# First layer of a two-layer streaming encoder: products of x times the norm's weight, the norm's factor multiplied onto the product tiles, and another order of gates and y products

## The chip, the cores and the metric

The kernel runs on one core of a Trainium2 chip. The metric is the device time of one execution in microseconds. TensorE does the matmuls, ScalarE the activation functions, VectorE elementwise work and scans, GpSimd elementwise work; SyncE issues most DMAs. Each engine works through its own list of instructions in order; between engines there are semaphores.

## What is computed

The reference runs two layers for 1024 frames of a new stream and 64 frames of a running one. Only the first layer's mixer is touched here:

```python
def rmsnorm(x, g):
    y = x * rsqrt(mean(x * x, axis=-1) + 1e-6)
    return y * g

def lru_mixer(h, conv_buf, h0, ...):          # h = rmsnorm(x, norm_mix[0])
    gate = gelu(h @ w_y + b_y)
    u, new_buf = causal_dwconv(h @ w_x + b_x, conv_buf, conv_w, conv_b)   # 4 taps
    r = sigmoid(block_diag(u, ga_w, ga_b))
    i = sigmoid(block_diag(u, gx_w, gx_b))
    log_a = -8.0 * r * softplus(-lam)
    a = exp(log_a)
    bx = sqrt(-expm1(2.0 * log_a)) * (i * u)
    hs = scan(h_t = a_t * h_{t-1} + bx_t), starting from h0
    return (hs * gate) @ w_out + b_out, new_buf, hs[:, -1]
```

Behind it come a residual, a causal ConvFFN, a second layer (RWKV-7 mixing and another ConvFFN) and a last norm. All sizes are fp32: D_MODEL 1024, so 8 channel tiles of 128.

## The kernel before

Activations lie transposed: a tile is 128 channels by 1092 columns (1024 frames, 4 columns of gap, 64 frames), and x is 8 such tiles (X). A matmul takes 364 columns, so a tile is three. Each fp32 product is made of three: operands are split into a high part and a rest (`WH`, `WL` for weights, `HH`, `HL` for rows of h, `PH`, `PL` for rows going into the output projection). ScalarE writes the high parts (`w_hi`, `h_hi`, `p_hi`), GpSimd the rests of weights and of the projection's rows (`w_lo`, `p_lo`), VectorE the rests of h. An **up product** (`up`, L1236) is one tile of output: 8 tiles of input by 3 parts by 3 column blocks, 72 matmuls. A **down product** is one output tile of the projection for two channel tiles: 18 matmuls; `down` (L1263) makes eight. Products go in turn into two accumulators in PSUM, `ACC[0]` and `ACC[1]`; who has emptied one says so with `taken0` or `taken1`, and TensorE waits for that before it writes there again.

The head (before the first product): SyncE issues four small priming loads, the vectors V, the constants CO, the eight tiles of x, and two weight tiles (L332 to L340). `norm` on ScalarE (L510) squares each x tile as it lands, VectorE adds the squares up (L1698), TensorE sums over channels with a matrix of ones (L1275), ScalarE takes the root by Ln and Exp. Then `h_rows` (L1715) on VectorE writes x times weight times factor, ScalarE the high part, VectorE the rest, and `up_two` (L1244) makes the first two x products together, tile by tile.

The recurrent block runs in four groups of two channel tiles, f = 2g and 2g+1. In a group before, TensorE made: x product, x product, y product, gates of f, y product, gates of f+1, and from group 1 on the eight down products of the group before (g-1). `gates` (L1303) are two products of a 128 by 128 block by the convolved tile, in full fp32. ScalarE empties x products into `UB` (row 0 of T, with bias), y products through Gelu into rows 2 and 3, and the gate products through Sigmoid into rows 4 and 5; behind the sigmoids come Tanh, Exp and Sqrt, each with a table load. VectorE runs `lru_conv` (L1780: three one-column copies of history, a copy of the state, a TENSOR_SCALAR and three taps), `drive` (gate times convolved tile), `scale` (two steps behind the root), `run_on` (fill, copy, scan), `gated` (a copy of the state and the product of scan and y tile), and takes the down products onto X (`take`, L1734). Rows of T are shared by the channels (R, I, S, Q are rows 4 to 7), so ScalarE waits for `conv` or `p_lo` before it overwrites one. Weights come through two buffers: a weight is loaded when `w_lo` of the one before the last is done, and its high part is written once the product that used the buffer is finished.

The later norm, ahead of the first layer's ConvFFN, is already made the other way: products of x times weight, and the factor `RS` multiplied onto the product tiles; `inverse_root` (L533), `scaled_hi` (L529), `scaled_lo` (L1709) and `sums_of_squares` (L1287) belong to it.

## Time and profile before

| | us |
|---|---|
| three runs, median | 3187.39 |
| lowest, highest | 3183.47, 3194.0 |
| the profiled execution | 3185.53 |
| its span | 3183.7 |
| TensorE busy in the span | 3013.1 |
| end of the touched stretch (sum of squares of the next norm) | 408 |

The profile is of one execution. Its timeline gives each instruction or run of like instructions with start and length, and in brackets how long the engine was idle before and what ended that. The table of stretches gives busy times between two points in time and the clock that TensorE was granted (1.0 is 2.4 GHz, 0.5 is 1.2 GHz). The groups add up instructions of a line and shape.

### The profile page before, as it was taken

To read this page: it belongs to the slowest core of one execution; us is meant where nothing else is said; L and a number is where in the kernel's file an instruction comes from. 1 tells how busy PE (TensorE), PEld (TensorE's weight loads), DVE (VectorE), ACT (ScalarE), POOL (GpSimd) and SP (SyncE) were. 2 spreads that over 40 slices of the span, in tenths; PEclk is the share of its full clock that TensorE was granted. 3 is DMA by queue.
4 is the path that set the end of the run, shared out by engine and by line. 5 is a ranking of instruction groups with operands and counts; after the bars stand their busy time and mean duration, and the time that the engine had idled before them with its cause. 6 is when DMAs were issued, how large, how long until landed. Compare 5 with 4: busy or idle time off the path is not lost.

```text
span 3183.7 us, 66664 instructions
## 1 busy us (share of the span) xinstructions
PE 3013.1 (95%) x29240; PEld 2894.2 (91%) x29240; DVE 1760.1 (55%) x1821; ACT 1027.6 (32%) x1269; POOL 968.3 (30%) x549
## 2 busy tenths in 40 slices
PE   6999899999999999879997999998999999999997
PEld 5898899999999999879996777887999999999996
DVE  5555665556555557512205777773566555555566
ACT  4633521111111112544315777774311111111112
POOL 1222122222322224313313555652132222222221
PEclk9999999999999999999998999999999999999998
DMA  3111011111111111052232222212111111111111
GB/s 104 37 43 44 27 47 41 47 41 46 41 47 47 41 47 40 28 217 89 83 123 63 72 72 70 72 50 97 48 41 48 40 47 47 41 47 41 46 47 63
DMA packets 87531, 185.65 MB, mean 58 GB/s; under 512 B 28896, under 2 KB 51936, under 8 KB 87264
## 3 DMA queue, kind: packets, MB, share of 16 engines
q1 hardware_dynamic: 80352, 154.73, 15.4%
q10 hardware_dynamic: 6912, 26.84, 2.1%
q8 instruction: 231, 3.78, 0.5%
q14 instruction: 36, 0.29, 0.0%
HBM read 145.01 MB, written 36.53 MB: 57 GB/s over the span
## 4 chain that ended last, share of the span: by engine, by line
PE 79%; DVE 12%; ACT 5%; issue 1%; POOL 1%; DMA 1%; ACTq 0%; SPq 0%; DVEq 0%; POOLq 0%
PE PS L1230 66%; PE PS L1426 9%; DVE T L1676 2%; DVE X L1676 2%; PE PS L1361 2%; DVE T L1691 2%; ACT T L492 1%; DVE BK L1676 1%; PE PS L1258 1%; DVE HL L1686 1%; DVE G L1676 1%; ACT UV L492 1%; ACT L492 1%; DVE T L1681 1%; DVE T L1686 1%
## 5 line engine op out<-in xcount | busy, mean ns | idle before, releaser
L1011 POOL TENSOR_TENSOR WL<-RAW,WH 128x1024 fp32r<-128x1024 f32 x204 | 497.4, 2438 | 1454.9 <-ACT WH L492 1451.0
L1230 PE MATMUL PS<-HH,WH 128*128 128x364 f32 x3408 | 757.6, 330 | 28.1 <-DVE HL L1676 12.5
L1230 PE MATMUL PS<-HH,WL 128*128 128x364 f32 x3408 | 756.5, 330 | 0.0
L1230 PE MATMUL PS<-HL,WH 128*128 128x364 f32 x3408 | 752.9, 329 | 0.0
L1230 PEld LDWEIGHTS PS<-HH,WH 128*128 128x128 f32 x3408 | 591.7, 188 | 36.4 <-DVE HL L1676 12.2
L1230 PEld LDWEIGHTS PS<-HH,WL 128*128 128x128 f32 x3408 | 596.9, 189 | 0.0
L1230 PEld LDWEIGHTS PS<-HL,WH 128*128 128x128 f32 x3408 | 593.8, 189 | 0.0
L492 ACT ACTIVATE WH<-RAW 128x1024 fp32r<-128x1024 f32 x204 | 216.5, 1061 | 766.2 <-PE PS L1230 752.8
L1676 DVE TENSOR_TENSOR X<-PS,X 128x1092 f32<-128x1092 f32 x224 | 290.1, 1295 | 234.2 <-PE PS L1230 228.4
L1676 DVE TENSOR_TENSOR T<-PS,T 128x1092 f32<-128x1092 f32 x96 | 124.3, 1295 | 529.3 <-PE PS L1230 517.3
L1230 PE MATMUL PS<-PH,WH 128*128 128x364 f32 x1344 | 300.8, 332 | 20.8 <-ACT T L492 7.8
L1230 PE MATMUL PS<-PL,WH 128*128 128x364 f32 x1344 | 298.3, 330 | 0.0
L1230 PE MATMUL PS<-PH,WL 128*128 128x364 f32 x1344 | 298.0, 330 | 0.0
L1011 POOL TENSOR_TENSOR PL<-T,PH 128x1092 fp32r<-128x1092 f32 x56 | 144.6, 2582 | 403.5 <-ACT PH L492 402.3
L1686 DVE SCALAR_TENSOR_TENSOR T<-T,FP 128x1092 f32<-128x1092 f32 x192 | 260.3, 1356 | 6.8
L1230 PEld LDWEIGHTS PS<-PH,WH 128*128 128x128 f32 x1344 | 232.5, 189 | 32.3 <-DVE X L1676 14.5
L1230 PEld LDWEIGHTS PS<-PH,WL 128*128 128x128 f32 x1344 | 235.2, 189 | 0.0
L1230 PEld LDWEIGHTS PS<-PL,WH 128*128 128x128 f32 x1344 | 233.9, 189 | 0.0
L492 ACT ACTIVATE PH<-T 128x1092 fp32r<-128x1092 f32 x56 | 62.6, 1118 | 464.5 <-DVE T L1676 463.5
L1691 DVE COPY T<-FP 128x2 f32<-128x2 f32 x96 | 207.8, 2165 | 3.3
L1676 DVE TENSOR_TENSOR T<-T 128x1092 f32<-128x1092 f32 x100 | 143.7, 1437 | 43.8 <-ACT T L492 37.2
L492 ACT ACTIVATE T<-T 128x1092 f32<-128x1092 f32 x61 | 68.2, 1117 | 307.2 <-DVE T L1686 307.1
(175 smaller groups left out, 3383.2 us busy)
## 6 DMA issues: line engine op xcount, KB each, us to landing
RAW<-weights SPq DMA_DIRECT2D x204, 512.0 KB, 3.4
scratch<-T ACTq DMA_DIRECT2D x31, 546.0 KB, 3.2
scratch<-SR ACTq DMA_DIRECT2D x14, 546.0 KB, 2.9
X<-xT SPq DMA_DIRECT2D x8, 546.0 KB, 7.5
yT<-HF SPq DMA_DIRECT2D x8, 546.0 KB, 2.9
T<-scratch_m SPq DMA_DIRECT2D x8, 512.0 KB, 4.4
KK<-scratch SPq DMA_DIRECT2D x16, 192.0 KB, 2.9
LW<-scratch SPq DMA_DIRECT2D x16, 192.0 KB, 2.7
```

The lines of the kernel that those rows point to most:

```text
L492: act.activation(out, in_, func, bias=bias, scale=scale).then_inc(*t.made(event, n))
L1011: pool.tensor_tensor(out, full, hi, ALU.subtract).then_inc(*t.made(event))
L1230: mm = pe.matmul(acc[:, j, :], a, b[:, j * CW:(j + 1) * CW], start=(i == 0 and q == 0), stop=(i == len(blocks) - 1 and q == 2))
L1258: mm = pe.matmul(acc[:, j, :], a[:, k, :], b[:, k, j * CW:(j + 1) * CW], start=(k == 0 and i == 0), stop=(k == KT - 1 and i == 2))
L1361: mm = pe.matmul(acc[:, j, :], w, x[:, k, j * CW + c:(j + 1) * CW + c], start=(k == 0 and i == 0), stop=(k == KT - 1 and i == 5))
L1426: mm = pe.matmul(out, lhsT, rhs, start=first, stop=True, skip_group_check=True)
L1676: dve.tensor_tensor(out, a, b, op).then_inc(*t.made(event, n))
L1681: dve.tensor_scalar(out, a, s1, s2, op1, op2).then_inc(*t.made(event))
L1686: dve.scalar_tensor_tensor(out=out, in0=a, scalar=s, in1=b, op0=op1, op1=op2).then_inc(*t.made(event, n))
L1691: dve.tensor_copy(out, a).then_inc(*t.made(event))
```

## The change

- **Head.** No scaled rows in the first layer. SyncE issues V, weight 0, the x tiles, weight 1, CO and only then the priming loads. ScalarE writes the high part of x times `mix0` as each tile lands, VectorE the rest (`scaled_lo`), and TensorE makes the two x products one after the other with `up`; the first takes the tiles as they come. Squares go to rows of T behind that; the sum over channels comes behind the second x product, its root goes to `RL` (row 7).
- **Factor.** x product tiles and y product tiles are multiplied by `RL` by VectorE, straight out of PSUM (`scaled`, `y_in`), and VectorE, not ScalarE, releases their accumulators. In group 0 ScalarE copies the two x products out first, and VectorE multiplies these copies. Gelu then works in place on the y tile. The x bias is folded into the convolution's bias and the history (11 short operations once, one more copy of 3 columns in each convolution).
- **Order.** From group 1 on TensorE makes x, x, gates of f, y, gates of f+1, y, down products. In group 0 it is x, x, sum of squares, y, gates, y, gates. VectorE does both gated steps late, the second one behind the first addition of the down products' tiles. Scan results go to `LS`, two rows (6, and row 0 which was UB), y tiles to `LY`.
- **ScalarE and GpSimd.** In groups 1 to 3 one weight split stands behind each channel's square root and the two `p_hi` stand together ahead of the last two; GpSimd's list follows.

The diff, cut to its core (of loops, only the new lines and what stays):

```diff
-M_LRU = 1
+M_LRU = 0
...
+        RL = T[:, 7, 0:COLS]
+        LR, LI = T[:, 4, 0:COLS], T[:, 5, 0:COLS]
+        LS = [T[:, 6, 0:COLS], T[:, 0, PAD:ROW]]
+        LY = [T[:, 2, 0:COLS], T[:, 3, 0:COLS]]
+        SQ = [T[:, r, 0:COLS] for r in (3, 1, 2, 4, 5, 1, 2, 4)]
...
+            sp.dma_start(V[:, :], io["vectors"]).then_inc(*t.made("dma_vec"))
+            weight(0)
+            for k in range(KT):
+                sp.dma_start(X[:, k, :], io["xT"][k]).then_inc(*t.made(f"dma_x{k}"))
+            weight(1)
+            sp.dma_start(CO[:, :], io["consts"][:, 0:C_LV]).then_inc(*t.made("dma_const"))
             for j, name in enumerate(PRIMED):
                 sp.dma_start(PRIME[:, j, :], io["consts"][:, 0:2]).then_inc(sems[name], 16)
-            sp.dma_start(V[:, :], io["vectors"]).then_inc(*t.made("dma_const"))
-            sp.dma_start(CO[:, :], io["consts"][:, 0:C_LV]).then_inc(*t.made("dma_const"))
-            for k in range(KT):
-                sp.dma_start(X[:, k, :], io["xT"][k]).then_inc(*t.made(f"dma_x{k}"))
-            weight(0)
-            weight(1)
...
+            def gates(m, f):
+                if f:
+                    act.wait_ge(*t.at("post", 6 * f))
+                evacuate(m, row3(LR), ACT.Sigmoid, bias=vec("ga_b", f))
+                evacuate(m + 1, row3(LI), ACT.Sigmoid, bias=vec("gx_b", f))
+            def decay(f):
+                if f == 0:
+                    act.wait_ge(*t.next("vprep"))
+                    act.wait_ge(*t.at("raw_in", 1))
+                if f >= 2:
+                    act.wait_ge(*t.at("p_full", f - 1))
+                run(LS[f % 2], LR, ACT.Tanh, "tan", scale=DV[:, 8, f:f + 1])
+                run(LR, LR, ACT.Exp, "tan", scale=DV[:, 12, f:f + 1])
+                run(LS[f % 2], LS[f % 2], ACT.Sqrt, "root")
+            def gelu(m, f):
+                act.wait_ge(*t.at(f"taken{m % 2}", m // 2 + 1))
+                run(LY[f % 2], LY[f % 2], ACT.Gelu_apprx_tanh, "gelu", bias=vec("b_y", f))
+            m, n = M_LRU, 0
+            w_hi(0, 0)
+            for k in range(KT):
+                act.wait_ge(*t.at(f"dma_x{k}", 1))
+                scaled_hi(k, "mix0")
+            w_hi(1, 0)
+            for k in range(KT):
+                if k == 3:
+                    evacuate(m, row3(T[:, 0, PAD:ROW]), ACT.Copy)
+                if k >= 5:
+                    act.wait_ge(*t.at("summed", k - 4))
+                run(SQ[k], X[:, k, :], ACT.Square, "squared")
+            w_hi(2, m + 1)
+            act.wait_ge(*t.at("dma_const", 1))
+            run(DV[:, 13, 0:1], CO[:, 0:1], ACT.Ln, "primed")
+            evacuate(m + 1, row3(LS[0]), ACT.Copy)
+            w_hi(3, m + 2)
+            inverse_root(m + 1, RL)
+            gates(m + 3, 0)
+            decay(0)
+            w_hi(4, m + 3)
+            gelu(m + 2, 0)
+            p_hi(0, LY[0])
+            gates(m + 6, 1)
+            decay(1)
+            w_hi(5, m + 6)
+            gelu(m + 5, 1)
+            p_hi(1, LY[1])
+            m, n = m + 8, n + 4
+            for g in range(1, LRU_GROUPS):
...
                 w_hi(n + 2, m + 1)
+                gates(m + 2, f)
+                decay(f)
                 w_hi(n + 3, m + 2)
+                gates(m + 5, f + 1)
+                decay(f + 1)
+                w_hi(n + 4, m + 5)
+                gelu(m + 4, f)
+                gelu(m + 7, f + 1)
+                w_hi(n + 5, m + 8)
+                p_hi(slot, LY[0])
+                p_hi(slot + 1, LY[1])
                 m, n = m + 8, n + 4
+                w_hi(n + 2, m + 4)
+                w_hi(n + 3, m + 8)
+                m, n = m + KT, n + 2
...
+            w_lo(5)
+            p_lo(0, LY[0])
+            w_lo()
+            p_lo(1, LY[1])
+            for g in range(1, LRU_GROUPS):
                 slot = 2 * (g % 2)
-                w_lo()
-                if g:
-                    p_lo(3 - slot, S)
-                w_lo(3)
-                p_lo(slot, S)
-                if g:
-                    w_lo(2)
-            p_lo(slot + 1, S)
+                w_lo(4)
+                p_lo(slot, LY[0])
+                p_lo(slot + 1, LY[1])
+                w_lo(2)
...
+            up(m, n, fresh=True, alone=True)
+            up(m + 1, n + 1)
+            pe.wait_ge(*t.at("dma_const", 1))
+            pe.wait_ge(*t.at("taken0", 1))
+            t.n["squared"] = t.n["root_ln"] = 0
+            sums_of_squares(m + 2)
+            up(m + 2, n + 2)
+            gates(m + 3, 0)
+            up(m + 5, n + 3)
+            gates(m + 6, 1)
+            m, n = m + 8, n + 4
+            for g in range(1, LRU_GROUPS):
+                up(m, n)
+                up(m + 1, n + 1)
+                gates(m + 2, 2 * g)
+                up(m + 4, n + 2)
+                gates(m + 5, 2 * g + 1)
+                up(m + 7, n + 3)
+                m, n = down(m + 8, n + 4, g - 1)
...
+            for k in range(KT):
+                scaled_lo(k, "mix0")
+            for k in range(1, KT):
+                dve.wait_ge(*t.at("squared", k + 1))
+                tt(SQ[0], SQ[0], SQ[k], ALU.add, "summed")
+            t.n["squared"] = KT
...
+            def scaled(out, m):
+                dve.wait_ge(*t.at("acc_ready", m + 1))
+                tt(row3(out), ACC[m % 2], row3(RL), ALU.mult, f"taken{m % 2}", m // 2 + 1)
+            def lru_conv(f):
+                copy(UB[:, PAD - 3:PAD], DV[:, 9:12, f], "hist")
                 for j in range(3):
                     copy(UB[:, PAD + HIST - 2 + j:PAD + HIST - 1 + j], vec(f"lc{j}", f), "hist")
-                copy(ST[:, f, 0:6].rearrange("p (s c) -> p s c", s=2), tails(UB[:, PAD:], 3), "kept")
+                ts(ST[:, f, 0:6].rearrange("p (s c) -> p s c", s=2), tails(UB[:, PAD:], 3), CO[:, 0:1], vec("b_x", f),
+                   ALU.mult, ALU.add, "kept")
                 conv(UB, U[f % 2], [vec(f"cw{j}", f) for j in range(4)], vec("cb", f))
+            def y_in(m, f):
+                if f >= 2:
+                    dve.wait_ge(*t.at("p_lo", f - 1))
+                scaled(LY[f % 2], m)
...
+                dve.wait_ge(*t.next("gelu"))
+                tt(LY[f % 2], LS[f % 2], LY[f % 2], ALU.mult, "p_full")
...
             m = M_LRU
+            dve.wait_ge(*t.next("rstd"))
+            tt(UB[:, PAD:ROW], UB[:, PAD:ROW], RL, ALU.mult, "tap")
+            dve.wait_ge(*t.at("dma_const", 1))
+            lru_conv(0)
+            y_in(m + 2, 0)
+            dve.wait_ge(*t.at("taken1", 1))
+            tt(UB[:, PAD:ROW], LS[0], RL, ALU.mult, "raw_in")
+            lru_conv(1)
+            drive(m + 3, 0)
+            scale(0)
+            run_on(0)
+            y_in(m + 5, 1)
+            gated(0)
+            drive(m + 6, 1)
+            scale(1)
+            run_on(1)
+            gated(1)
+            m += 8
+            for g in range(1, LRU_GROUPS):
                 f = 2 * g
+                scaled(UB[:, PAD:ROW], m)
+                lru_conv(f)
+                scaled(UB[:, PAD:ROW], m + 1)
+                lru_conv(f + 1)
+                drive(m + 2, f)
                 scale(f)
                 run_on(f)
+                y_in(m + 4, f)
+                drive(m + 5, f + 1)
+                scale(f + 1)
+                run_on(f + 1)
+                y_in(m + 7, f + 1)
                 gated(f)
                 m += 8
+                for d in range(KT):
+                    if d == 1:
+                        gated(f + 1)
+                    take(m + d, d, vec("b_out", d) if g == 1 else None)
+                m += KT
```

ScalarE, group 1, from the gates of f=2 on, before (PS is the accumulators, V and DV vectors, RAW a weight as loaded, WH its high part):

```order
L492 ACTIVATE T_57<-PS,V_66 128x1092 [waits acc_ready]
L492 ACTIVATE T_57<-PS,V_66 128x1092 [waits taken0,acc_ready]
L492 ACTIVATE T_57<-T_57,DV_67 128x1092 [waits taken1]
L492 ACT_TABLE_LOAD
L492 ACTIVATE T_57<-T_57,DV_67 128x1092 [waits tan]
L492 ACT_TABLE_LOAD [waits tan]
L492 ACTIVATE T_57<-T_57 128x1092 [waits p_lo]
L492 ACT_TABLE_LOAD [waits root]
L492 ACTIVATE T_57<-PS,V_66 128x1092 [waits acc_ready]
L492 ACTIVATE WH1_62<-RAW1_60 128x1024 [waits taken0,acc_ready,dma_w1]
L492 ACTIVATE PH_54<-T_57 128x1092 [waits w_hi,p_full]
```

And in the changed kernel, from the gates of f=2 to the high parts of the gated tiles (L497 is `run`, L492 before):

```order
L497 ACTIVATE T_57<-PS,V_66 128x1092 [waits post]
L497 ACTIVATE T_57<-PS,V_66 128x1092 [waits taken0,acc_ready]
L497 ACTIVATE T_57<-T_57,DV_67 128x1092 [waits taken1,p_full]
L497 ACT_TABLE_LOAD
L497 ACTIVATE T_57<-T_57,DV_67 128x1092 [waits tan]
L497 ACT_TABLE_LOAD
L497 ACTIVATE T_57<-T_57 128x1092 [waits tan]
L497 ACTIVATE WH1_62<-RAW1_60 128x1024 [waits root,acc_ready,dma_w1]
L497 ACT_TABLE_LOAD [waits w_hi,acc_ready]
```

Before, no weight split stood between the square root and the next Gelu load, and the split was ahead of the gates block; now a split of the weight comes right behind the square root, and the Gelus are gone from the gates.

VectorE, group 1, behind the convolution of f=3, before (X is the residual, SR the convolved tile of odd channels, ST the state):

```order
L1691 COPY ST_74<-T_57 128x2 [waits post]
L1676 TENSOR_TENSOR T_57<-T_57 128x1092 [waits kept]
L1676 TENSOR_TENSOR T_57<-T_57,SR_77 128x1092 [waits p_full,taken0]
L1686 SCALAR_TENSOR_TENSOR X_49<-PS,V_66,X_49 128x1092 [waits post,acc_ready]
L1686 SCALAR_TENSOR_TENSOR X_49<-PS,V_66,X_49 128x1092 [waits taken1,acc_ready]
L1686 SCALAR_TENSOR_TENSOR T_57<-T_57 128x1092 [waits taken0,root]
L1676 TENSOR_TENSOR T_57<-T_57 128x1092 [waits post]
L1686 SCALAR_TENSOR_TENSOR X_49<-PS,V_66,X_49 128x1092 [waits post,acc_ready]
L1696 MEMSET T_57 128x1 [waits taken1]
```

And in the changed kernel, from the y tile of f=3 on:

```order
L1692 TENSOR_TENSOR T_57<-PS,T_57 128x1092 [waits post,acc_ready,p_lo]
L1707 COPY ST_74<-T_57 128x2 [waits taken1]
L1692 TENSOR_TENSOR T_57<-T_57 128x1092 [waits kept,gelu]
L1702 SCALAR_TENSOR_TENSOR X_49<-PS,V_66,X_49 128x1092 [waits p_full,acc_ready]
L1707 COPY ST_74<-T_57 128x2 [waits taken0]
L1692 TENSOR_TENSOR T_57<-T_57 128x1092 [waits kept,gelu]
L1702 SCALAR_TENSOR_TENSOR X_49<-PS,V_66,X_49 128x1092 [waits p_full,acc_ready]
L1702 SCALAR_TENSOR_TENSOR X_49<-PS,V_66,X_49 128x1092 [waits taken1,acc_ready]
```

The first addition onto X stands behind the gated step of f=2 now, and the second behind that of f=3; the multiply of the y tile out of PSUM stands ahead of both.

## Rows read from the trace of the kernel before

**Rows 1.** The page, part 1: busy time, share of the span, instructions.
```profile
PE 3013.1 (95%) x29240; PEld 2894.2 (91%) x29240; DVE 1760.1 (55%) x1821; ACT 1027.6 (32%) x1269; POOL 968.3 (30%) x549
```

**Rows 2.** Timeline of the head: start, length (us), engine, line, operation, [idle before].
```profile
0.76 1.82 SPq L332 DMA_DIRECT2D PRIME<-consts  x4
...
7.62 1.11 ACT L492 ACTIVATE T<-X 128x1092 f32<-128x1092 f32 x1 [1.35 <-DMA X<-xT]
...
8.97 0.38 DVE L1681 TENSOR_SCALAR DV<-DV 128x8 f32<-128x8 f32 x2
...
17.73 1.11 ACT L492 ACTIVATE T<-X 128x1092 f32<-128x1092 f32 x1 [0.25 <-DMA X<-xT]
...
31.67 1.25 PE L1258 MATMUL PS<-HH,WH 128*128 128x364 f32 x3 [6.22 <-ACT HH L492]
```

**Rows 3.** Table of stretches, TensorE: busy (matmuls), granted clock, DMA share, GB/s.
```profile
31.67:37.00 5.33, 5.33 (x18) 0.50 0.00 0
...
62.18:67.90 5.72, 5.72 (x19) 0.50 0.31 92
...
160.50:163.50 3.00, 2.92 (x10) 0.50 0.50 186
...
364.87:368.90 4.03, 4.03 (x14) 0.53 0.03 5
...
100.77:187.82 87.05, 81.90 (x456) 0.98 0.15 47
187.82:358.63 170.81, 160.84 (x913) 1.00 0.12 39
```

**Rows 4.** Timeline of TensorE, first layer: matmul rows behind waits, gates, sum of squares.
```profile
62.18 1.28 PE L1230 MATMUL PS<-HH,WH 128*128 128x364 f32 x3 [3.61 <-POOL WL L1011]
...
82.26 0.74 PE L1230 MATMUL PS<-HH,WH 128*128 128x364 f32 x3 [1.39 <-ACT T L492]
...
94.34 3.83 PE L1311 MATMUL PS<-SR,GW 128*128 128x364 f32 x12
...
100.77 0.74 PE L1230 MATMUL PS<-HH,WH 128*128 128x364 f32 x3 [2.60 <-ACT T L492]
...
364.87 1.28 PE L1230 MATMUL PS<-PH,WH 128*128 128x364 f32 x3 [6.24 <-POOL PL L1011]
...
408.04 2.21 PE L1292 MATMUL PS<-T,CO 128*128 128x68 f32 x6 [2.44 <-DVE T L1676]
```

**Rows 5.** Groups by form, 0 to 400 us: busy us, mean ns | idle before.
```profile
L492 ACT ACT_TABLE_LOAD x36 | 46.2, 1283 | 2.7 <-PEq L2264 0.7
...
L492 ACT ACTIVATE T<-PS,V 128x1092 f32<-128x1092 f32 x32 | 37.5, 1173 | 113.1 <-PE PS L1230 89.5 <-DVE T L1686 15.4 <-PE PS L1258 7.4
...
L1676 DVE TENSOR_TENSOR X<-PS,X 128x1092 f32<-128x1092 f32 x24 | 31.1, 1296 | 25.9 <-PE PS L1230 24.8
...
L492 ACT ACTIVATE WH<-RAW 128x1024 fp32r<-128x1024 f32 x26 | 27.5, 1059 | 56.0 <-PE PS L1230 53.8
...
L1804 DVE TENSOR_TENSOR_SCAN T<-T 128x1092 f32<-128x1092 f32 x8 | 19.5, 2432 | 0.3
...
L492 ACT ACTIVATE T<-T,DV 128x1092 f32<-128x1092 f32 x16 | 19.3, 1209 | 0.4
...
L1681 DVE TENSOR_SCALAR SR<-T,V 128x1092 f32<-128x1092 f32 x4 | 3.4, 848 | 0.1
```

**Rows 6.** Timeline of VectorE and of GpSimd, convolutions of f=2 and f=4.
```profile
117.98 3.21 DVE L1681 TENSOR_SCALAR T<-T,V 128x1092 f32<-128x1092 f32 x1
...
121.22 4.14 DVE L1686 SCALAR_TENSOR_TENSOR T<-T,V 128x1092 f32<-128x1092 f32 x3
...
118.06 2.54 POOL L1011 TENSOR_TENSOR PL<-T,PH 128x1092 fp32r<-128x1092 f32 x1
...
205.31 3.44 POOL L1011 TENSOR_TENSOR PL<-T,PH 128x1092 fp32r<-128x1092 f32 x1
...
202.94 3.38 DVE L1686 SCALAR_TENSOR_TENSOR T<-T,V 128x1092 f32<-128x1092 f32 x1
```

136 lines of the change are left out of this document (27 added, 109 removed).

## The prediction

> **What bounds the kernel now.** TensorE is busy for 3013 of 3183.7 us [rows 1], so I looked for the time in which it waits, and only in the stretch that the change touches: the head and the first layer's recurrent block, up to 408 us. The timeline of the head [rows 2] shows the long wait: the first product starts at 31.67 us. Ahead of it stand eight square passes paced by the loads of x (7.62 to 18.84, the rows 1.44 us apart), the adding up, the norm's sum, its root, and only then the scaled rows. The table of stretches [rows 3] gives two more things. Group 1 (100.77 to 187.82) takes 87.05 us and TensorE is busy in 81.9 of them; groups 2 and 3 take 85.4 us each, busy 80.4. And four stretches stand at granted clock 0.50, that is 1.2 GHz, where the rest runs at 2.4: behind the cold start, and behind idle times of 3.61, 2.60 and 6.24 us (the second of these at 160.50; the same 2.60 at 100.77 did not bring it). Half clock costs half its length: 2.66 us in the first of them, 2.86 in the second, 1.5 and 1.9 in the last two. The matmul rows [rows 4] show where TensorE waits inside a group: 1.39 and 2.60 us behind each pair of gate products, where the next product wants an accumulator that ScalarE still empties, and 6.24 us ahead of the last down products, for ScalarE's and GpSimd's split of the last channel.
>
> **Durations I use** [rows 4 to 6]: an up product 12.05 us (from 82.26 to the gate pair at 94.34), a gate pair 3.83, one down product 3.03 (18 matmuls, an up product 72); ScalarE 1.17 to evacuate, 1.06 for a weight split, 1.28 for a table load, 1.21 for a decay pass; VectorE 1.30 for a 1092-wide operation of two tensors, 2.43 for the scan; GpSimd 2.2 to 2.5 for a split. The hop from engine to engine is 0.1 to 0.2.
>
> **A lock.** The rows of a convolution [rows 6] show what else VectorE pays. Undisturbed its three taps take 4.14 us, so a whole convolution, with the TENSOR_SCALAR of 0.85 and its short copies, is 5.8. At 202.94 one tap takes 3.38 instead of 1.38 while GpSimd works, and at 117.98 a TENSOR_SCALAR of 0.85 takes 3.21: it ends 0.6 after GpSimd does. The other way round GpSimd's subtraction takes 3.44 at 205.31, where it asked in the middle of a tap, and it then goes ahead of VectorE's next tap. So each operation of VectorE on tensors in SBUF waits for GpSimd's running one, and between two of them a waiting GpSimd wins. The additions from PSUM onto X were not lengthened.
> The Trainium skill ("SBUF — State Buffer", section "SBUF: two separate sides") says that the port pair shared by the two engines is an exclusive lock, held for the whole instruction, and that it touches VectorE instructions with two SBUF inputs or in a two-port mode. The trace agrees (3.38 against 1.38), and by that rule the new multiplies out of PSUM, which read one tensor of SBUF, never wait; if they did, each of the four in a group could cost another 2.2 us, but only one of them comes while GpSimd works.
>
> **A. The head and group 0.** V goes out first, 1.86 us earlier than before (four PRIME issues stand behind), then weight 0, then x. Row 0 of x landed at 7.6; less 1.86, plus 1.35 for weight 0 (512 KB at the pace of x, 546 KB in 1.44), less 0.5 for CO (192 KB), gives 6.6 [rows 2]. Weight 0, just ahead of it and the first large load, is there by some 4.8; its high part at 5.8, its low part at 8.2. VectorE's chain of small operations (ending at 9.35 before, and 2.5 earlier now) would end at 6.9, but GpSimd's split falls into it, so 9.2; the low part of row 0 at 10.6. The product starts at **10.65** instead of 31.67. Low parts follow every 1.44 us (a tap's 1.38 and the hop), the eight blocks of the product take an eighth of 12.05 each, twice that at half clock, so TensorE doesn't starve. From here by addition: x product 0 ends at 25.3 (12.05 + 2.66 for half clock, as behind 31.67), x product 1 at 37.35, the sum of squares 39.55 (2.21 at 408.04 [rows 4]). Its cover: squares, interleaved with the evacuation at 25.3, end at 32.6, VectorE's adds at 34. TensorE then waits for the first root piece, which stands on ScalarE behind the evacuation of product 1 and a weight split: 40.25. The factor is there at 43.65, the multiply of x tile 0 and its convolution end at 51.0, under the y product (40.25 to 52.3): hidden. Gates to 56.1, y product 1 to 68.2. Then the new costs. The second gate matmul of f=1 needs the accumulator of y product 1, which VectorE now empties; VectorE stands in scale and scan. ScalarE's root ends at 63.65, the weight split right behind it releases GpSimd at 64.8, in the middle of VectorE's first scale step, so GpSimd takes the lock at 65.05 and the second step ends at 68.35 instead of 66.4; scan 71.15, multiply 72.55: TensorE waits **2.5**. Gates end at 74.5. ScalarE's next sigmoid stands behind the high part of gated channel 0 (there at 74.1): 75.3, table load 76.6, sigmoid 77.85. TensorE waits **3.45**, and group 1 begins at 77.95 instead of 100.77: **+22.8**.
>
> **B. Group 1.** Gated channel 1 ends at 94.4 (root at 85.35, the lock, scan), and its high part on ScalarE stands ahead of the next weight split. Both low parts on GpSimd (95.65 to 100.6) meet the convolution of f=2, as at 115 to 121 before; it ends at 105.35, where the x products end at 102.05: wait 3.35 (half clock behind the 3.45 would hide in this). Then, as in every group: wait 2.5 at the second gate matmul of the odd channel (scale, lock, scan, y multiply); wait 1.3 at down product 1, for the y multiply of the last product; and down product 3 waits for the second addition, which now stands behind both gated steps: the state copy waits for GpSimd's weight split (148.9), then the low part takes the lock to 151.5, the gated multiply ends at 152.65, the addition at 154.05, down product 2 having ended at 150.15: wait 3.95. Sum: 80.4 + 3.35 + 2.5 + 1.3 + 3.95 = 91.5 against 87.05: **-4.4**.
>
> **C. Groups 2 and 3.** The convolution of the even channel meets one GpSimd split and ends at 20.9 us of the group, ahead of the x products' 24.1: hidden. The old waits of 1.39 and 2.60 and some 1.1 in the down products go; 2.5 + 1.3 + 3.95 come. 80.4 + 7.75 = 88.15 against 85.4, twice: **-5.5**.
>
> **D. Last down products.** Channel 7 is split long before; the wait of 6.24 and its half clock (1.9) go: **+8.1**. What follows (VectorE's chain to 408) is as before.
>
> **E. Clock.** The waits of 3.95 are as long as the 3.61 that brought half clock, those of 2.5 as the 2.60 that brought it once. I charge one such drop, the mean of 1.5 and 2.86: **-2**. Bounds: none, and all of them (below).
>
> Sum: 22.8 - 4.4 - 5.5 + 8.1 - 2 = **19.0** us. Against the profiled execution's 3185.5: 3166.5. The median of the three runs is 3187.4, 1.9 above it, their spread 10.5; the rest of the program is untouched.
>
> **Rivals.**
> 1. The lock is not lost at the handover: VectorE's second scale step and the gated multiply start before the waiting GpSimd. For it: no row shows this pair of instructions; against it: 205.31 and 118.06. Then 2.5 becomes 0.5, 1.3 nothing, 3.95 some 1.5: groups 2 and 3 take 82.4 (+6.0), group 1 85.75 (+1.3), the head gains 24.7 (its 2.5 becomes 0.6), D stays 8.1: gain 40.1, time **3145**. Chance 0.20.
> 2. Every wait from 2.4 us up brings half clock of 5.7 us: two in each of three groups, 6 x 2.86 = 17.2 instead of 2: gain 3.8, time **3182**. For it the row at 62.18; against it three of four waits of 2.60 without. Chance 0.12.
> 3. Slower: half clock stays for the down products. If the two waits at down products 1 and 3 keep the clock at 1.2 GHz through the eight products, each costs 3.03 more: 24.2 a group, 73 in three, time **3240**. It decides the sign from 10.2 us a group (20 us at half clock), where 21.0 + 9.6 are used up. Against it: no stretch at half clock in the trace is longer than 5.8 us. Chance 0.03.
> 4. The change doesn't start early: x and weight 0 land late or VectorE's low parts are held by GpSimd, up to 5 us of the 21 at the start. That only shifts: 3171, within my case.
> My own case has 0.65; by its terms it reaches from 3154 (waits of the down products half as long, no drop) to 3176 (head 4 later, three drops).
>
> **Numbers.** The range 3145 to 3180 takes in my case, rival 1 down to its centre, and the near side of rival 2. A measurement of this kernel can tell about 0.3% (9.6 us). Faster by more than that: 0.65 + 0.20 and a little of rival 2, 0.86; same 0.11; slower 0.03.
>
> **What would show it.** In the profile after: first product near 10.65 and the first x product of group 1 near 78; waits of TensorE for VectorE's T (y multiply) of about 2.5, 1.3 and one near 4 for X in each group; GpSimd's split of 3.4 us or a scale step of 3.3 right behind the square root; no wait ahead of the last down products. It is wrong if the second scale step takes 1.30 everywhere, if groups 2 and 3 take under 84 us or above 92, or if a granted clock of 0.5 covers more than some 15 us behind 60 us.

## The result, and the profile after

| | before | after |
|---|---|---|
| median of the runs side by side (4 and 4) | 3190.69 | 3166.19 |
| lowest, highest | 3183.47, 3195.43 | 3163.91, 3170.64 |
| the profiled execution | 3185.53 | 3163.91 |
| its span | 3183.7 | 3162.0 |
| end of the touched stretch | 408.04 | 385.24 |

The ratio is 0.9927, with a 95% interval of 0.9916 to 0.9938: 24.5 us between the medians, 21.6 between the profiled executions, 22.8 in the touched stretch, where 19.0 were forecast. The time forecast was 3166.5, in a range of 3145 to 3180. One execution of a later repeat (r1_after) took 3681.39 us at a granted clock of 0.747, and counts in no ratio and no median below. TensorE has nearly the work of [rows 1]; of the 21.7 us that went from the span, 17.8 are its idle time (170.6 to 152.8) and 3.9 its busy time:

```profile
PE 3009.2 (95%) x29234; PEld 2890.9 (91%) x29234; DVE 1790.2 (57%) x1848; ACT 1017.7 (32%) x1261; POOL 966.1 (31%) x549
```

The timeline of the kernel after is to be read beside [rows 2] and [rows 4]. First the head and group 0, TensorE's rows behind waits and what the first of them rests on (start, length, engine, line, operation, [idle before]):

```profile
5.62 1.06 ACT L497 ACTIVATE WH<-RAW 128x1024 fp32r<-128x1024 f32 x1 [2.00 <-DMA RAW<-weights]
...
6.76 2.35 POOL L1042 TENSOR_TENSOR WL<-RAW,WH 128x1024 fp32r<-128x1024 f32 x1 [6.30 <-ACT WH L497]
...
8.22 14.27 DVE L1702 SCALAR_TENSOR_TENSOR HL<-X,V,HH 128x1092 fp32r<-128x1092 f32 x8 [1.54 <-ACT HH L497]
...
10.41 1.25 PE L1259 MATMUL PS<-HH,WH 128*128 128x364 f32 x3 [10.41 <-DVE HL L1702]
...
72.20 2.10 PE L1319 MATMUL PS<-SR,GW 128*128 128x364 f32 x6 [2.73 <-DVE T L1692]
77.60 1.25 PE L1259 MATMUL PS<-HH,WH 128*128 128x364 f32 x3 [3.30 <-ACT T L497]
```

The first product starts at 10.41 instead of 31.67, and group 1 at 77.60 instead of 100.77: 23.2 us. The first low part of x (the first of the eight from 8.22) could only get going when GpSimd's split had ended at 9.11. Then the waits of group 1, and the same wait at the end of group 2:

```profile
105.55 3.94 PE L1319 MATMUL PS<-T,GW 128*128 128x364 f32 x12 [2.37 <-DVE T L1702]
...
107.72 1.28 ACT L497 ACT_TABLE_LOAD   x1 [11.31 <-PE PS L1319]
...
110.33 0.74 PE L1259 MATMUL PS<-HH,WH 128*128 128x364 f32 x3 [0.84 <-ACT T L497]
...
126.76 2.10 PE L1319 MATMUL PS<-SR,GW 128*128 128x364 f32 x6 [2.37 <-DVE T L1692]
...
145.41 0.77 PE L1259 MATMUL PS<-PH,WH 128*128 128x364 f32 x3 [1.52 <-DVE T L1692]
...
153.21 0.77 PE L1259 MATMUL PS<-PH,WH 128*128 128x364 f32 x3 [1.45 <-DVE X L1702]
...
241.33 0.78 PE L1259 MATMUL PS<-PH,WH 128*128 128x364 f32 x3 [1.49 <-DVE X L1692]
```

Each PE row is one wait of TensorE, in the order of the program (the row of 107.72 is ScalarE's, and is taken up further down): the convolution of f=2, the sigmoid behind the even gates, the y multiply that frees the accumulator for the second odd gate, the y multiply at down product 1, the addition at down product 3. Groups 2 and 3 have the last four of them (sigmoid 0.85 and 0.85, y multiply 2.37 and 2.36, down product 1 1.45 and 0.84, down product 3 1.49 and 1.43). The group borders are 77.60, 168.23, 256.37 and 343.88, so the groups take 90.6, 88.1 and 87.5 us. Ahead of the last down products there is no wait in place of the 6.24 [rows 4], and the stretch to the sum of squares is 8.1 us shorter.

Table of stretches of TensorE, to be read beside [rows 3] (busy, granted clock, DMA share, GB/s):

```profile
77.60:80.00 2.40, 2.40 (x8) 0.50 0.00 0
...
213.36:217.00 3.64, 3.64 (x7) 0.55 0.00 0
...
301.48:304.40 2.92, 2.92 (x7) 0.67 0.02 6
...
168.40:344.10 175.70, 164.08 (x914) 0.98 0.12 38
```

Half clock (1.2 GHz) comes behind the idle time of 3.30, and behind two of the six of 2.36 to 2.73 (at 72.20, 105.55, 126.76, 213.36, 301.48, and the 2.44 ahead of the sum of squares at 385.24).

### The profile page after: what moved, and what is told of

The parts are those of the page before. It is cut to its first block, busy times and chain, and to the rows that moved or that the text cites. A ratio compares the mean times of both kernels' runs of the same rounds, so it can differ in the third digit from the quotient of the medians.

```text
span 3162.0 us, 66636 instructions
## 1 busy us (share of the span) xinstructions
PE 3009.2 (95%) x29234; PEld 2890.9 (91%) x29234; DVE 1790.2 (57%) x1848; ACT 1017.7 (32%) x1261; POOL 966.1 (31%) x549
## 4 chain that ended last, share of the span: by engine, by line
PE 78%; DVE 14%; ACT 6%; issue 1%; POOL 1%; DMA 1%; ACTq 0%; SPq 0%; DVEq 0%; POOLq 0%
PE PS L1259 65%; PE PS L1442 9%; DVE T L1692 3%; ACT T L497 2%; DVE T L1707 2%; PE PS L1377 2%; DVE X L1692 2%; ACT L497 1%; DVE BK L1692 1%; DVE T L1702 1%; DVE HL L1702 1%; DVE G L1692 1%; DVE T L1697 1%; ACT UV L497 1%; PE PS L1319 1%
## 5 line engine op out<-in xcount | busy, mean ns | idle before, releaser
L1259 PE MATMUL PS<-HH,WH 128*128 128x364 f32 x3456 | 771.4, 331 | 33.2 <-DVE HL L1702 12.7
L1259 PE MATMUL PS<-HH,WL 128*128 128x364 f32 x3456 | 767.9, 331 | 0.0
L1259 PE MATMUL PS<-HL,WH 128*128 128x364 f32 x3456 | 764.6, 330 | 0.0
L1259 PEld LDWEIGHTS PS<-HH,WH 128*128 128x128 f32 x3456 | 601.7, 189 | 43.0 <-issue 22.2
L1259 PEld LDWEIGHTS PS<-HH,WL 128*128 128x128 f32 x3456 | 606.2, 189 | 0.0
L1259 PEld LDWEIGHTS PS<-HL,WH 128*128 128x128 f32 x3456 | 603.3, 189 | 0.0
L497 ACT ACTIVATE WH<-RAW 128x1024 fp32r<-128x1024 f32 x204 | 216.6, 1062 | 779.0 <-PE PS L1259 763.7
L1692 DVE TENSOR_TENSOR T<-PS,T 128x1092 f32<-128x1092 f32 x110 | 142.6, 1296 | 555.1 <-PE PS L1259 542.0
L497 ACT ACTIVATE PH<-T 128x1092 fp32r<-128x1092 f32 x56 | 62.6, 1117 | 484.3 <-DVE T L1692 484.0
L1692 DVE TENSOR_TENSOR T<-T 128x1092 f32<-128x1092 f32 x103 | 164.8, 1600 | 14.7 <-ACT T L497 7.0
L497 ACT ACTIVATE T<-T 128x1092 f32<-128x1092 f32 x61 | 68.2, 1118 | 307.2 <-DVE T L1702 307.0
```

The lines of the kernel that those rows point to most:

```text
L497: act.activation(out, in_, func, bias=bias, scale=scale).then_inc(*t.made(event, n))
L1259: mm = pe.matmul(acc[:, j, :], a, b[:, j * CW:(j + 1) * CW], start=(i == 0 and q == 0), stop=(i == len(blocks) - 1 and q == 2))
L1692: dve.tensor_tensor(out, a, b, op).then_inc(*t.made(event, n))
```

## Experiments

The end of the touched stretch is the start of the sum of squares (L1302; 408.04 before) in the profiled execution. Medians are of 3 to 11 runs, taken beside 9 to 15 runs of the kernel before on the same chip (their medians 3189.2 to 3190.5). The number in front of a name is the set that it ran in: the kernels of set 2 had the kernel before beside them, but no kernel after, and are compared with r1_after.

| kernel | median | ratio to before, 95% | end of stretch |
|---|---|---|---|
| r1_after | 3163.4 | 0.9923 [0.9903, 0.9943] | 385.34 |
| r1_load_order | 3180.1 | 0.9971 [0.9958, 0.9983] | 399.21 |
| r1_old_order | 3166.9 | 0.9933 [0.9916, 0.9949] | 384.92 |
| r1_split_early | 3156.1 | 0.9896 [0.9879, 0.9912] | 371.19 |
| r2_late_rows | 3175.6 | 0.9955 [0.9938, 0.9971] | 392.99 |
| r2_copy_last | 3178.8 | 0.9965 [0.9951, 0.9979] | 396.92 |
| r2_take_first | 3162.5 | 0.9915 [0.9898, 0.9932] | 379.24 |
| r2_head_gates | 3167.6 | 0.9931 [0.9915, 0.9948] | 384.69 |
| r3_after | 3166.7 | 0.9916 [0.9902, 0.9929] | 384.17 |
| r3_before_loads | 3187.9 | 0.9991 [0.9982, 1.0000] | 407.33 |
| r3_two | 3153.9 | 0.9877 [0.9862, 0.9893] | 369.92 |
| r3_all | 3147.8 | 0.9864 [0.9848, 0.9879] | 366.20 |

The stretch is the finer measure, with two limits. In three executions of the kernel after it ends at 385.24, 385.34 and 384.17, so a difference of about 1 us says nothing. And it ends where the sum of squares starts, so half clock right behind that isn't in it. The kernel after and r3_after, which is the same kernel:

```profile
385.24 2.21 PE L1302 MATMUL PS<-T,CO 128*128 128x68 f32 x6 [2.44 <-DVE T L1692]
```

```profile
384.17 3.42 PE L1302 MATMUL PS<-T,CO 128*128 128x68 f32 x6 [2.43 <-DVE T L1692]
```

In the ten us from there on TensorE makes 54 matmuls at a granted clock of 1.00 in the first and 44 at 0.83 in the second, which is worth 1.7 us. r1_load_order, r1_old_order, r1_split_early, r2_copy_last, r2_take_first, r3_two and r3_all have it too (0.83 or 0.84); the kernel before, r1_after, r2_late_rows, r2_head_gates and r3_before_loads don't. The rest varies as well: from the end of the stretch to the same sum of squares in the second layer the kernel after takes 1893.7 us in one execution, 1890.9 in r1_after and 1898.2 in r3_after (385.24 to 2278.95, 385.34 to 2276.28, 384.17 to 2282.36), with not one instruction changed. So a median of four runs can differ from what the stretch says by a few us.

The kernel after, once in each of two sets, as what the others are compared with:

> The changed kernel itself, as the measure for the other three. Every theory expects what was measured: 21 to 25 us faster than before, first product near 10.4 us, group 1 from 77.6 us.

> The changed kernel once more, as the standard of this set. Both theories: ratio to before 0.9923, within its interval of 0.9903 to 0.9943; the second sum of squares (end of the touched stretch) starts at 385.2 to 385.4 us.

Both repeat the result: 385.34 and 384.17, ratios 0.9923 and 0.9916.

### Does the early start come from the order of the loads?

```diff
-            sp.dma_start(V[:, :], io["vectors"]).then_inc(*t.made("dma_vec"))
-            weight(0)
-            for k in range(KT): ...
-            weight(1)
-            sp.dma_start(CO[:, :], io["consts"][:, 0:C_LV]).then_inc(*t.made("dma_const"))
             for j, name in enumerate(PRIMED): ...
+            sp.dma_start(V[:, :], io["vectors"]).then_inc(*t.made("dma_vec"))
+            sp.dma_start(CO[:, :], io["consts"][:, 0:C_LV]).then_inc(*t.made("dma_const"))
+            for k in range(KT): ...
+            weight(0)
+            weight(1)
```

> The loads of the head in the order of before (priming, vectors, constants, x, weight 0, weight 1), all else as in the changed kernel. If the early start hangs on weight 0 standing ahead of x: it lands near 19, is split by 22.6, the first product starts there instead of at 10.41, and everything behind it shifts by some 12 us (time +12). Rival, the head is set by the norm's own chain (squares, adds, root), which has slack left: the products are late but the factor isn't, and less than 6 us of it is seen at the end.

And a part of that order in the kernel before: the priming loads go behind x and the weights, while V and CO stay ahead of x and weight 0 behind it:

```diff
-            for j, name in enumerate(PRIMED): ...
             sp.dma_start(V[:, :], ...)
             sp.dma_start(CO[:, :], ...)
             for k in range(KT): ...
             weight(0)
             weight(1)
+            for j, name in enumerate(PRIMED): ...
```

> The kernel before, with only the priming loads moved behind x and the weights (V, CO, x, weight 0, weight 1, then the priming loads). Theory that the early start needs both parts, loads and unscaled rows: the rows of x land 1.8 us earlier, the eight squares, the sum over channels and the root follow, and the first product starts at 29.9 instead of 31.67; the touched stretch gets 1.8 us shorter, which the median can't tell from none (ratio 0.9990 to 1.0010). Rival, that the order of loads alone brings the 14 us that it was worth in the changed kernel: first product near 17, ratio 0.9955.

Timelines of r1_load_order (weight split, GpSimd's split, first product) and of r3_before_loads (first product):

```profile
20.08 1.06 ACT L497 ACTIVATE WH<-RAW 128x1024 fp32r<-128x1024 f32 x1 [14.62 <-DMA RAW<-weights]
21.21 2.35 POOL L1042 TENSOR_TENSOR WL<-RAW,WH 128x1024 fp32r<-128x1024 f32 x1 [20.76 <-ACT WH L497]
24.86 1.25 PE L1259 MATMUL PS<-HH,WH 128*128 128x364 f32 x3 [24.86 <-DVE HL L1702]
```

```profile
30.41 1.25 PE L1258 MATMUL PS<-HH,WH 128*128 128x364 f32 x3 [6.22 <-ACT HH L492]
```

With weight 0 behind x, the weight is what the first product waits for, 14.4 us longer, and the whole of it reaches the end: 13.9 in the stretch, 16.7 in the median. In the kernel before the later priming loads alone are worth 1.3 us of the first product (30.41; 1.8 expected) and nothing that the median tells, since there the chain of squares and root ends last. So of the 21.3 us of the early start 6.8 come without the new order of loads (31.67 to 24.86), 1.3 with the priming loads moved alone, and the other 13.2 only came with unscaled rows and the whole new order together. The whole new order in the kernel before wasn't run; its first product stands behind the root, as the row above shows (it waits for the high part of the scaled rows), so an earlier weight 0 could hardly help there, but that is argued and not shown.

### Is the wait at the odd gates the lock?

The weight splits stand ahead of the gates' evacuations, so GpSimd's split no longer falls into `scale`:

```diff
                 w_hi(n + 2, m + 1)
+                w_hi(n + 3, m + 2)
                 gates(m + 2, f)
                 decay(f)
-                w_hi(n + 3, m + 2)
+                w_hi(n + 4, m + 5)
                 gates(m + 5, f + 1)
                 decay(f + 1)
-                w_hi(n + 4, m + 5)
```

> In groups 1 to 3 ScalarE's two weight splits that stand right behind a square root are moved ahead of the gates block before it, where ScalarE is idle; GpSimd's list is the same. If the lock is what costs: the second scale step takes 1.30 instead of 3.44 in six places, the waits of 2.37 fall to 0.5 or less and those of 1.45 go, the half clock behind the 2.37 goes, the convolution of the odd channel gets 2.3 longer under the gates and y product: 10 to 13 us faster than the changed kernel. Rival, the waits come from the y multiply standing behind scale and scan on VectorE, whatever GpSimd does: the waits stay within 0.5 of 2.37 and 1.45, time within 2 us.

The two steps of `scale` of f=2, in the kernel after, with GpSimd's split:

```profile
117.74 1.30 DVE L1702 SCALAR_TENSOR_TENSOR T<-T 128x1092 f32<-128x1092 f32 x1 [3.29 <-ACT T L497]
...
118.96 2.39 POOL L1042 TENSOR_TENSOR WL<-RAW,WH 128x1024 fp32r<-128x1024 f32 x1 [18.55 <-ACT WH L497]
119.07 3.43 DVE L1692 TENSOR_TENSOR T<-T 128x1092 f32<-128x1092 f32 x1
```

and in r1_split_early, with TensorE's row behind them and the end of the stretch:

```profile
118.15 1.29 DVE L1702 SCALAR_TENSOR_TENSOR T<-T 128x1092 f32<-128x1092 f32 x1 [2.67 <-ACT T L497]
119.48 1.29 DVE L1692 TENSOR_TENSOR T<-T 128x1092 f32<-128x1092 f32 x1
...
125.04 2.10 PE L1319 MATMUL PS<-SR,GW 128*128 128x364 f32 x6 [0.24 <-DVE T L1692]
...
371.19 3.89 PE L1302 MATMUL PS<-T,CO 128*128 128x68 f32 x6 [2.43 <-DVE T L1692]
```

The second step takes 1.29 instead of 3.43 and TensorE's wait falls from 2.37 to 0.24. The wait at down product 1 goes too, since the odd channel's steps were held by the same lock (3.45 at 137.70 in the kernel after). The stretch is 14.2 us shorter than r1_after's, the median 7.3. Of the 14.2, 1.7 are given back as half clock right behind the stretch; against r3_after, which has that too, the stretch is 13.0 shorter. So the lock at the handover, the point on which the forecast's own case and rival 1 parted, is there, and it cost the kernel after some 13 us in three groups, together with the half clock behind its waits: both have it from 77 to 125 us (granted clock 0.96), but r1_split_early then stands at 1.00 up to 344, where the kernel after has 0.96 from 210 to 256 and again from 300 to 347.

### What is the order "gates ahead of y" worth?

Groups 1 to 3 go back to x, x, y, gates, y, gates, down, with ScalarE's and VectorE's lists to match; the head, the factor, and the odd channel's high and low part ahead of the down products' weight splits stay:

```diff
-                gates(m + 2, 2 * g)
-                up(m + 4, n + 2)
-                gates(m + 5, 2 * g + 1)
-                up(m + 7, n + 3)
+                up(m + 2, n + 2)
+                gates(m + 3, 2 * g)
+                up(m + 5, n + 3)
+                gates(m + 6, 2 * g + 1)
```

> Groups 1 to 3 in the order of before (x, x, y, gates, y, gates, down products, the odd channel's scale, scan and gated step between the first additions); head and factor as in the changed kernel. If the order is what removed the wait ahead of the last down products: this wait of 6.24 and its half clock come back (+8), and behind the second gate pair TensorE waits 3.3 for a sigmoid that stands behind the high part, as in group 0 (+2.7 a group): +16 in all. Rival, the groups cost the same in either order since VectorE's and ScalarE's work is the same: +8 only, all of it ahead of the last down products.

TensorE's rows behind waits in its group 1:

```profile
132.07 2.10 PE L1319 MATMUL PS<-SR,GW 128*128 128x364 f32 x6 [0.56 <-DVE T L1692]
...
138.53 1.25 PE L1259 MATMUL PS<-PH,WH 128*128 128x364 f32 x3 [4.35 <-ACT T L497]
```

The small waits are smaller, and one of 4.35 stands where the down products follow the last gates and want an accumulator that ScalarE still has to empty behind the high part of the gated tile. That wait brings half clock (three matmuls in 1.25 instead of 0.74). The stretch ends at 384.92 against 385.34, with half clock behind it (1.7) that r1_after doesn't have: the order by itself is worth nothing that shows. Nor did the wait ahead of the last down products come back, so it can't have been the matmuls' order that removed it. The next kernel looks for what did.

### What removed the wait ahead of the last down products?

In the kernel after the high and low parts of both channels of a group stand ahead of the two weight splits of the down products. Here the odd channel's go behind them, on ScalarE and on GpSimd:

```diff
                 p_hi(slot, LY[0])
-                p_hi(slot + 1, LY[1])
                 m, n = m + 8, n + 4
                 w_hi(n + 2, m + 4)
                 w_hi(n + 3, m + 8)
+                p_hi(slot + 1, LY[1])
...
                 p_lo(slot, LY[0])
-                p_lo(slot + 1, LY[1])
                 w_lo(2)
+                p_lo(slot + 1, LY[1])
```

> The order of products as in the changed kernel, but in groups 1 to 3 the odd channel's high part and low part stand behind the two weight splits of the down stage on ScalarE and GpSimd, as before the change. If that list position made the wait of 6.24 us ahead of the last down products, it comes back with half clock: +8 in the touched stretch, nothing elsewhere. Rival, the order of gates and y products removed it (VectorE's gated step comes earlier): no wait there, time within 2 us of the changed kernel.

```profile
342.89 1.06 ACT L497 ACTIVATE WH<-RAW 128x1024 fp32r<-128x1024 f32 x1 [10.87 <-PE PS L1259]
344.03 2.35 POOL L1042 TENSOR_TENSOR WL<-RAW,WH 128x1024 fp32r<-128x1024 f32 x1 [9.53 <-ACT WH L497]
344.04 1.11 ACT L497 ACTIVATE PH<-T 128x1092 fp32r<-128x1092 f32 x1
346.51 2.48 POOL L1042 TENSOR_TENSOR PL<-T,PH 128x1092 fp32r<-128x1092 f32 x1
349.05 1.28 PE L1259 MATMUL PS<-PH,WH 128*128 128x364 f32 x3 [6.25 <-POOL PL L1042]
```

The wait is back, 6.25 against 6.24 before [rows 4], with half clock behind it, and the stretch is 7.7 us longer (median 12.1). The chain reads from top to bottom: the weight split can only be made when the product that used the buffer is finished (ScalarE idle for 10.87), the high part of channel 7 stands behind it, the low part behind GpSimd's split of the weight. The data of channel 7 had long been there. What the change gained here is a place in two lists.

### Where did the wait of 3.95 go?

The forecast put 3.95 on down product 3, with GpSimd's low part taking the lock ahead of the gated multiply; 1.45 was measured. The two engines in the kernel after:

```profile
147.85 2.40 POOL L1042 TENSOR_TENSOR WL<-RAW,WH 128x1024 fp32r<-128x1024 f32 x1 [7.86 <-ACT WH L497]
...
148.46 1.82 DVE L1707 COPY ST<-T 128x2 f32<-128x2 f32 x1
150.38 1.30 DVE L1692 TENSOR_TENSOR T<-T 128x1092 f32<-128x1092 f32 x1
150.39 6.34 POOL L1042 TENSOR_TENSOR PL<-T,PH 128x1092 fp32r<-128x1092 f32 x2
```

The state copy waits out GpSimd's split, as forecast (1.82 instead of 0.17). But then it is over in an instant, and the multiply starts at 150.38, while GpSimd's next instruction asks at 150.39. That the multiply comes first is no toss: at the nine such places of three executions (the kernel after, r1_after, r3_after) it started 0 to 20 ns ahead each time. To see what happens when GpSimd asks first, the copy goes behind the multiply, in `gated`:

```diff
-                copy(ST[:, f, 6:8]...., tails(LS[f % 2], 1), "kept")
                 dve.wait_ge(*t.next("gelu"))
                 tt(LY[f % 2], LS[f % 2], LY[f % 2], ALU.mult, "p_full")
+                copy(ST[:, f, 6:8]...., tails(LS[f % 2], 1), "kept")
```

> In the gated step the product comes first and the two-column copy of the state behind it. The prediction's wait of 3.95 at down product 3 was 1.45. If it hung on who gets the lock between a copy and a multiply: the multiply now waits for the weight split, and the waiting low part of GpSimd takes the lock ahead of the copy, so that the addition is held: wait at down product 3 near 3.5 in each of three groups, +6 us. Rival, GpSimd's low part doesn't matter there: wait 1.2 to 1.5, no change.

```profile
148.28 2.88 DVE L1692 TENSOR_TENSOR T<-T 128x1092 f32<-128x1092 f32 x1
150.14 6.01 POOL L1042 TENSOR_TENSOR PL<-T,PH 128x1092 fp32r<-128x1092 f32 x2
...
151.19 2.34 DVE L1707 COPY ST<-T 128x2 f32<-128x2 f32 x1
...
155.05 0.77 PE L1259 MATMUL PS<-PH,WH 128*128 128x364 f32 x3 [3.57 <-DVE X L1702]
```

Now the multiply waits for the split and goes first (it ends at 151.16), GpSimd asks at 150.14, in the middle of it, and takes the lock ahead of the copy, which takes 2.34. The addition behind the copy is late by that much, and down product 3 waits 3.57, 3.59 and 3.54 in the three groups. The forecast's mechanism exists, then; in the kernel after it missed by 10 ns. The stretch got 11.6 us longer. Three times 2.1 is 6.3 of that. For the rest the table of stretches shows half clock behind these waits, where the kernel after had none (clock 1.00 from 153 to 162, from 241 to 250 and from 328.8 to 334). In r2_copy_last:

```profile
153.00:162.00 9.00, 6.95 (x32) 0.81 0.05 18
246.00:253.00 7.00, 6.38 (x29) 0.76 0.00 0
337.00:345.00 8.00, 7.15 (x27) 0.58 0.01 3
```

By slices of some 45 us the clock from 125 to 347 us costs r2_copy_last 10.1 us (43 at 0.96, 46 at 0.93, 47 at 0.89, the others 1.00) and the kernel after 3.7 (46 and 47 at 0.96): 6.4 more, which with the 6.3 makes 12.7 for the 11.6 measured, as near as hundredths of a clock allow.

### Taking first, and the head

In r2_take_first the second gated step stands behind the second addition of the down products:

```diff
-                    if d == 1:
+                    if d == 2:
                         gated(f + 1)
```

> The second addition onto X stands ahead of the odd channel's gated step, not behind it. If the wait of 1.45 at down product 3 is this addition being late: it goes in three groups, 4 us less in the touched stretch. Rival, the wait moves to down product 4: no gain.

The wait at down product 3 is gone in every group (3 times 1.45 is 4.4). The stretch is 6.1 us shorter, of which 1.6 are given back as half clock right behind it; the median is 0.9 us shorter, which the intervals don't tell from nothing. In r2_head_gates ScalarE empties the gates of channel 1 ahead of the high part of gated channel 0:

```diff
             gelu(m + 2, 0)
-            p_hi(0, LY[0])
             gates(m + 6, 1)
+            p_hi(0, LY[0])
             decay(1)
```

> In group 0 ScalarE empties the gates of f=1 ahead of the high part of channel 0. The wait of 3.30 ahead of group 1 goes, and the half clock behind it. If VectorE's chain for channel 1 and the convolution of f=2 set the time in group 1, as the prediction says, the wait ahead of the gates of f=2 grows from 2.3 to some 5, and only 1.9 us are gained, what the root of channel 1 comes earlier. Rival: the 3.3 and the 1.4 of half clock are both gained, 4.7.

```profile
103.94 5.62 PE L1319 MATMUL PS<-T,GW 128*128 128x364 f32 x12 [4.32 <-DVE T L1702]
```

The 3.30 ahead of group 1 went, and came back as 4.32 instead of 2.37 ahead of the gates of f=2, with half clock (5.62 for 12 matmuls instead of 3.94). VectorE's chain ends last there (gated step of channel 1, y multiply, and two lock waits, in a copy of 2.36 and a state step of 1.95, ahead of the taps of f=2). It ended 1.6 us earlier than in the kernel after, not 3.3, and the half clock took that (5.62 - 3.94 = 1.7). Stretch 384.69 against 385.34.

### Two versions that put the findings together

r3_two is split_early with take_first:

> The changed kernel with both one-place edits: the weight splits of the gates stand ahead of the gates' evacuations (as in r1_split_early) and the second gated step of a group stands behind the second addition (as in r2_take_first). Alone they shortened the touched stretch by 14.2 and 6.1 us. If they act on different waits: 20.3 together, second sum of squares at 365. If they share the wait ahead of down product 3 (my theory: without GpSimd's split in the way, that wait was already down to 0.8 in each of three groups): 2.4 more than the first alone, at 368.8, ratio 0.9890.

369.92: 1.3 us less than r1_split_early alone, which is about what one kernel differs by from itself, and 14.3 less than r3_after (12.7 in the median); ratio to before 0.9877. The two share their wait, as expected; what is left at down product 3 is 0.65 where 0.88 was. r3_all adds the head's order and an early table load:

```diff
                 w_hi(n + 3, m + 2)
+                run(DV[:, 13, 0:1], CO[:, 0:1], ACT.Sigmoid, "primed")
                 gates(m + 2, f)
...
             decay(0)
-            w_hi(4, m + 3)
             gelu(m + 2, 0)
-            p_hi(0, LY[0])
+            w_hi(4, m + 3)
             gates(m + 6, 1)
+            p_hi(0, LY[0])
             decay(1)
-            w_hi(5, m + 6)
             gelu(m + 5, 1)
+            w_hi(5, m + 6)
             p_hi(1, LY[1])
```

> The two edits of r3_two, and in group 0 the Gelu of channel 0 ahead of the weight split and the evacuation of both gates of channel 1 ahead of the high part of gated channel 0, and in groups 1 to 3 a sigmoid of one column ahead of the gates' evacuation, so that its table is loaded while ScalarE waits. Expected against r3_two: the wait of 0.85 behind each even gate pair falls to 0.1 or less (3 times 0.75), and of the head's 3.3 + 2.4 half stays (2.5 to 3): second sum of squares at 364, ratio 0.9880. Rival, that waits of group 0 only move into group 1 (as in r2_head_gates): 366.5, and no difference from r3_two that the median can tell.

```profile
88.45 1.28 PE L1260 MATMUL PS<-HH,WH 128*128 128x364 f32 x3 [4.00 <-POOL WL L1043]
...
107.51 0.74 PE L1260 MATMUL PS<-HH,WH 128*128 128x364 f32 x3 [0.42 <-ACT T L497]
```

366.20, 3.7 us less than r3_two, between the two numbers expected; ratio 0.9864 [0.9848, 0.9879], median 3147.8, the fastest of all: 42.7 us under the kernel before and 18.9 under the one after. The wait behind each even gate pair is 0.42 instead of 0.85: 1.3 us in three groups. In the head r3_two waited 2.72, 2.78 and, for the convolution, 2.40; here it is 0.57 and none and none, but a wait of 4.00 comes for a weight's low part that is now made later, with half clock behind it. The gates of f=2 start at 103.26 instead of 105.46, so 2.2 us are left.

## Why the prediction was right, step by step

The mechanisms came as told; how near the time came (3166.2 measured, 3166.5 forecast) is in part luck. The forecast was counted down from one execution of 3185.5, while the median of the kernel before was 3190.7, and the stretch gained 22.8 and not 19.0. Between the profiled executions, 3185.5 and 3163.9, the forecast is 2.6 us off.

- **A, the head: right, 23.2 against 22.8.** First product 10.41 against 10.65, group 1 at 77.60 against 77.95, the waits 2.73 and 3.30 against 2.5 and 3.45. One thing in it was otherwise than told: VectorE's small chain was not held by GpSimd's split. It ended at 6.68, and the split, behind a weight that landed 0.8 later than told, began at 6.76. It made no difference, because the low part of row 0 was held instead.
- **B, group 1: 90.6 against 91.5.** The wait for the convolution is 2.37 against 3.35, the y multiply 2.37 against 2.5, down product 1 1.52 against 1.3, all near. Two terms are off, and go against each other. 3.95 at down product 3 was **mis-sized**: it is 1.45, for the 10 ns shown above. And a wait of 0.84 behind the even gates was **missed**. Its cause is in the rows of 107.72: ScalarE had idled for 11.31 us, yet the sigmoid's table load starts only when the gate product is ready, and the 1.28 come in front of the evacuation. An idle ScalarE was taken for a ready one. r3_all, where the table is loaded in that idle time, has 0.42.
- **C, groups 2 and 3: 88.1 and 87.5 against 88.15.** The waits at the odd gates and at down product 1 came as told (2.37 and 1.45 in group 2), but the sum is right by chance: 0.85 + 2.37 + 1.45 + 1.49 in group 2 is 6.2, not 7.75, and half clock adds 1.6 (3.64 us at 0.55).
- **D, last down products: 8.1 of 8.1.** The mechanism stood too ("channel 7 is split long before"), and r2_late_rows shows it to be the lists of ScalarE and GpSimd alone.
- **E, clock: 3.4 us lost against 2.** Read from the stretches: 3.64 times 0.45 and 2.92 times 0.33, and some 0.8 in the next 2.6 us behind 304.4 (clock 0.71). How many drops come is not fixed: in r3_after the matmuls behind the same wait at 301.37 run at full pace, and those behind 384.17 at half. The 1.5 behind 77.60 hides in the wait for the convolution, as B said.
- **Rival 1** (the lock isn't lost, 3145) is wrong for `scale`, where 3.43 to 3.45 was measured at every one of its places in groups 0 to 3, and right for one step, the gated multiply, by its timing. **Rival 2** (half clock behind every wait from 2.4 up): two of the six waits of 2.36 to 2.73 had it, four did not (2.10 to 2.21 for six matmuls, 3.94 for twelve). **Rival 3** (half clock through the down products): in r2_copy_last, with waits of the forecast length at that place, the matmuls are at half pace from 337.85 to 343.47 and at full pace behind that, so no. The reason given against it, that no stretch of the trace at half clock is longer than 5.8 us, is true of the touched stretch only: in the second layer of the kernel before the clock is 0.50 from 1680 to 1693, from 1697 to 1710 and from 2175 to 2188. **Rival 4** did not come.
- The touched stretch gained 22.8 and not 19.0: +0.4 in A, +0.8 in B, +2.7 in C with E (4.8 lost, 7.5 charged).

The Trainium skill ("SBUF — State Buffer", section "SBUF: two separate sides") says that where a VectorE instruction with two SBUF inputs meets a GpSimd instruction that reads SBUF, whichever starts first gets the port pair for its whole length. That rule and the rows at 150.38 and 150.39 agree, and by it the sign of those 10 ns decides a wait of 2.1 us in three groups.

## What to carry to other kernels

Where two engines share a lock, write down for each long operation what the other one is doing at that moment, and look for the trigger: here a weight split behind each square root cost some 13 us in three groups, and moving it ahead of the gates gave them back. A wait for data that "had long been there" is often a place in a list, so look at what stands ahead of the splitting instruction before changing the order of the matmuls. And a gain at the start reaches the end only when nothing that is bound elsewhere (the convolution chain in group 1) stands in between: 14.4 us of the head passed through, 3.3 us did not.

## What the runs showed of the hardware

Small operations of VectorE take part in the lock, but not all of them. Timeline of the convolution of f=2 in the kernel after:

```profile
95.32 2.55 POOL L1042 TENSOR_TENSOR PL<-T,PH 128x1092 fp32r<-128x1092 f32 x1 [6.76 <-ACT PH L497]
95.53 2.37 DVE L1707 COPY T<-DV 128x3 f32<-128x3 f32 x1
97.93 0.53 DVE L1707 COPY T<-V 128x1 f32<-128x1 f32 x3
98.01 2.39 POOL L1042 TENSOR_TENSOR WL<-RAW,WH 128x1024 fp32r<-128x1024 f32 x1
98.50 1.94 DVE L1697 TENSOR_SCALAR ST<-T,CO,V 128x6 f32<-128x6 f32 x1
```

A copy of three columns takes 2.37 (0.17 undisturbed) and a TENSOR_SCALAR of six 1.94 (0.29), each to the end of GpSimd's operation. Three copies of one column run through in 0.53 while GpSimd works, and so did the addition out of PSUM at 147.07 (1.35, with GpSimd's split from 147.85). The three columns of history that the change copies anew in every convolution are held for 2.37 here, and for 2.27 in groups 2 and 3, where the wait is hidden. That doesn't make them the cost: in the kernel before, without this copy, a copy of six columns (2.15 at 115.79) and the TENSOR_SCALAR behind it [rows 6] were held in the same place, and the convolution took 10.14 us (115.22 to 125.36) against 9.97 here (95.53 to 105.50). Whichever operation comes first waits. No run leaves the copy out.

Half clock is not settled by the idle time ahead of it: 2.37 us was followed by it at 213.36 (0.55) and not at 126.76, where six matmuls took 2.10. Nor is it settled by the kernel: ahead of the sum of squares 2.44 us of idle time went without it in one execution, and 2.43 us in another execution of the same kernel brought it (the two rows at the head of the experiments). What tells the cases apart is left open. For who measures, it means that a difference of 1 to 2 us between two executions can be one such drop.
